# The gate matmul of both layers as seven quadrant products, with the partial sums left in PSUM, and a shorter lead in the second mixer's output projection

## The chip, the cores and the metric

One Trainium2 chip, one of its cores. The metric is the device time of one execution in microseconds (us). A core has TensorE (PE in the profile; PEld is its weight load), VectorE (DVE), ScalarE (ACT), GpSimd (POOL) and SyncE (SP, which here only issues DMAs). All of them run their own queue in order and wait on semaphores for each other. SBUF is the on-chip working memory, PSUM the eight banks into which TensorE writes.

## The reference

Two layers over 1024 tokens of width 1024. The part of the reference that the change touches, cut down:

```python
def short_conv_mixer(x, w_in, conv_w, w_out):          # layer 1 only
    gate_b, gate_c, h = jnp.split(jnp.einsum('bsd,de->bse', x, w_in), 3, axis=-1)
    z = gate_c * h
    conv = sum(conv_w[k] * zp[:, k:k + s] for k in range(CONV_WIDTH))   # zp: z padded
    return jnp.einsum('bse,ed->bsd', gate_b * conv, w_out)

for i in range(DEPTH):
    mix = ...                                           # layer 0: pooling + gMLP, layer 1: short_conv_mixer
    x = layer_norm(DEEPNORM_ALPHA * x + mix, ln1_g[i], ln1_b[i])
    hid = jnp.square(jax.nn.relu(jnp.einsum('bsd,df->bsf', x, ffn_w1[i])))
    x = layer_norm(DEEPNORM_ALPHA * x + jnp.einsum('bsf,fd->bsd', hid, ffn_w2[i]), ln2_g[i], ln2_b[i])
    gate = jax.nn.sigmoid(jnp.einsum('bsd,de->bse', x, ple_gate_w[i]))
    x = x + gate * jnp.einsum('bsk,kd->bsd', p[i], ple_w[i])
```

The last two lines are the gate stage, run once per layer: a 1024x1024 by 1024x1024 product under a sigmoid, times a product of p (1024x256) with ple_w (256x1024).

## The kernel before

Every float32 matmul is made of three: each operand is split into a high part (fp32r) and the low rest, and `product` issues high by high, low by high and high by low into one PSUM bank. ACT makes a high part (a cast), DVE or POOL makes the low part (raw minus high, a `TENSOR_TENSOR`). Eight PSUM banks form two rings of four, `bank_a` and `bank_b`.

The whole program is a list of stages made by `make_plan`; each engine walks the same list and does its own share of each stage. The order of the work on an engine is thus the order of the plan. The large products (both FFN matmuls, most of the short convolution's input projection and its output projection) are already done as seven products of quadrants where a plain scheme has eight: `m1`, `m2`, `m7`, `m6`, `m5`, `m3`, `m4`. In the output projections `m6`, `m5` and `m3` are added in PSUM on top of `m1`, and `m4` on top of `m7`. A product of these is cut into items (`prod`); DVE and ACT make an item's operands ahead in `prep` (tiles `hop_hi`, `hop_lo`, `wop_hi`, `wop_lo`), up to five items ahead, and DVE drains the banks into `resid` when a product is done (L2153, L2156).

The gate stage before (`gates`) is plain: for each of the two column halves and each of the eight token tiles, PE makes eight `product`s of the gate (24 matmuls of 128x512) into one bank of ring B and two of p (6 matmuls) into the next. ACT takes the sigmoid (`sig`), DVE scales and shifts `resid` by the layer norm's rows `gb_rows` (L2339, L2340), multiplies sigmoid and p's product (L2344) and adds them to `resid` (L2347). The weights come by DMA into `raw`, ACT makes `w_hi` or `g_hi`, POOL `w_lo` or `g_lo` (L1326). TensorE transposes (L2404) make the x operands `xt_hi`, `xt_lo` of the second token half within this stage, and those of the next stage at its end.

Of the kernel before, what the change touches and what calls it, by code (L numbers as in the profile page):

```python
# [65 lines left out]
OD_DIRECT = {2: "g11", 3: "g21"}  # L66
PLE = 256
# [20 lines left out]
class Stage:  # L88
# [30 lines left out]
    def n(self, name, k=0):  # L119
# [20 lines left out]
    "alpha": {}, "affine": {},  # L140
    "vln": {}, "stats": {}, "norm": {}, "split": {}, "square": {}, "second": {}, "wsum": {}, "slab": {}, "more": {}, "gload": {}, "gsplit": {}, "p": {}, "psum_in": {}, "psum": {}, "psum_out": {}, "lasthid": {}, "tsum": {}, "thi": {}, "t4": {}, "step": {},
# [3 lines left out]
                h="conv", ffn="aval", out="bread", wide="bread", v="bread", gate="bread", prod="flu")  # L145

# [232 lines left out]
def make_plan():  # L379
# [9 lines left out]

    def add(kind, slab=None, last=False, **args):  # L390

        if slab is not None:
            slabs.append((slab, at["piece"]))
            at["slab"] += 1
            at["piece"] += 5 if slab[0] == "gate" else 4
# [22 lines left out]
        for ring, name in (("A", "ga"), ("B", "gb")):  # L418
            for k in range(adds.get(name, 0)):
                bank = (at[name] + k) % RING  # L420
                st.bank_before[ring].append(held[ring][bank])
                held[ring][bank] = (by, at[by] + k + 1)
# [10 lines left out]
        return st  # L433

# [59 lines left out]
    def ffn(layer):  # L494
# [35 lines left out]
        for i, (form, j) in enumerate(ITEMS):  # L530
# [26 lines left out]
            if i == LAST_FORM + 4:  # L557
                add("turn_p", half=0, layer=layer)
            if i == LAST_FORM + 5:
# [19 lines left out]
    def gates(layer):  # L579
        add("more", slab=("gate", layer, 0), split_next=False, load_next=False)  # L580
        add("gate", slab=("gate", layer, 1), tiles=[0, 1], layer=layer, split_next=False, load_next=False)
        add("gload", layer=layer)
        inner = [turns("ln", 1, list(range(KT)), ln=2 * layer + 1, nested=True)]
        inner.append(add("turn_p", half=1, layer=layer, nested=True))
        add("gate", tiles=[2, 3], inner=inner, layer=layer)
        add("gsplit", item=0, layer=layer)
        add("gate", tiles=hi[:-1], layer=layer)
        add("gsplit", item=1, layer=layer)
        add("gate", tiles=hi[-1:], layer=layer)
        for _ in range(3):  # L590
            slab_end.append(("gb", at["gb"]))
        for c in (2, 3):
            add("more", slab=("gate", layer, c), split_next=False, load_next=False)
        st = add("gate", tiles=lo, col=1, layer=layer, split_next=True, load_next=True)
        if layer == 0:
            last_half("gate", "gate", layer=layer, col=1)
        else:
            add("gate", tiles=hi, col=1, layer=layer, last=True)


    def short_conv():
# [28 lines left out]
        for i, (form, j) in enumerate(OD_ITEMS):  # L630
            while nxt < len(OD_ITEMS) and (a.user_before(nxt) is None or a.user_before(nxt) < i):
# [58 lines left out]
def trunk(nc, x, p, ev_w_in, ev_pool_w, ev_pool_scale, ev_sgu_ln_g, ev_sgu_ln_b, ev_sgu_w, ev_sgu_b, ev_w_out,  # L690
# [10 lines left out]
    with ExitStack() as ctx:  # L701
# [9 lines left out]
        def at(name, shape, offset, dt=F32):  # L711
# [4 lines left out]
            if offset + size > ARENA:  # L716
# [16 lines left out]
        sig = at("sig", [P, 2, HALF], 200 * K1)  # L733
        g_hi = [at(f"g_hi{k}", [P, PIECE], a * K1, F32R) for k, a in enumerate((152, 156, 160, 164, 168, 172))]
        g_lo = [at(f"g_lo{k}", [P, PIECE], a * K1, F32R) for k, a in enumerate((154, 158, 162, 166, 170, 174))]
# [18 lines left out]
                  for k, where in enumerate((104, 114, 124, 134, 200, 202, 204))]  # L754
# [79 lines left out]
        sig_ready = sem("sig_ready")  # L834
# [33 lines left out]
        gate_step = sem("gate_step")  # L868
# [8 lines left out]
                      odstep=od_step, odcopy=od_copied)  # L877
# [1753 lines left out]
```

## Time and profile before

| | us |
|---|---|
| median of 3 runs | 2071.99 (2071.43 to 2072.64) |
| the profiled execution, its own time | 2070.66 |
| its span, first to last instruction | 2068.9 |
| PE busy | 2052.1, 99% of the span, 9437 matmuls |
| DVE busy | 1325.2, 64% |
| ACT busy | 853.9, 41% |
| POOL busy | 790.2, 38% |
| granted TensorE clock, mean | 0.999 of full speed |

Busy time counts an instruction from its start to its modelled end, so that neighbouring matmuls overlap. The profiled execution's time lies 1.76 us over its span, and 1.33 us under the median.

### The profile page before, as it was taken

What the parts mean: (1) busy time and instruction counts of PE and PEld (TensorE: products, weight loads), DVE (VectorE), ACT (ScalarE), POOL (GpSimd) and SP (SyncE); (2) the same over time, 40 slices, a digit from 0 to 9 for tenths busy, and PEclk for the clock granted to TensorE, in tenths of its full rate; (3) what the DMA queues carried; (4) which work ended last, traced back from release to release, by engine and by line L of the source; (5) the groups of instructions that cost most, each with busy time, mean ns of one, the idle gap of its engine ahead of it and who ended that gap; (6) DMA issues with size and microseconds to landing.
All of it is one profiled execution on the core that took longest, in us unless ns stands there. A gap on an engine that the chain in (4) does not pass through costs nothing. (4 is left out here: it accounts for less than half of the span.)

```text
span 2068.9 us, 25147 instructions
## 1 busy us (share of the span) xinstructions
PE 2052.1 (99%) x9437; PEld 1702.7 (82%) x9437; DVE 1325.2 (64%) x1677; ACT 853.9 (41%) x1241; POOL 790.2 (38%) x523
## 2 busy tenths in 40 slices
PE   9999999999999999999999999999999999999999
PEld 9888788888888888888878887888888888888887
DVE  4744775655666757564687769775655666666563
ACT  3112465454544334431433334655445543334430
POOL 5212157787702000212266751167877412000220
PEclk9999999999999999999999999999999999999999
DMA  5111123444589655411022238034444599554221
GB/s 189 42 62 45 38 82 137 144 161 156 197 309 390 218 201 182 141 34 41 21 88 86 87 133 299 1 122 145 150 158 142 205 382 362 185 202 153 97 87 41
DMA packets 190708, 306.05 MB, mean 148 GB/s; under 512 B 13472, under 2 KB 71932, under 8 KB 190588
## 3 DMA queue, kind: packets, MB, share of 16 engines
q1 hardware_dynamic: 189888, 304.14, 42.1%
q8 instruction: 75, 1.23, 0.2%
q14 instruction: 45, 0.37, 0.1%
q10 hardware_dynamic: 700, 0.31, 0.1%
HBM read 233.62 MB, written 70.78 MB: 147 GB/s over the span
## 5 line engine op out<-in xcount | busy, mean ns | idle before, releaser
L1326 POOL TENSOR_TENSOR w_lo<-raw,w_hi 128x512 fp32r<-128x512 f32 x92 | 131.0, 1455 | 744.0 <-ACT w_hi L1441 744.0
L1339 POOL TENSOR_TENSOR op_lo<-op_sum,op_hi 128x512 fp32r<-128x512 f32 x151 | 225.1, 1506 | 34.4 <-ACT op_hi L1643 28.5
L1608 ACT CAST hop_hi<-h_raw 128x1024 fp32r<-128x1024 f32 x124 | 130.4, 1051 | 257.0 <-PE bank_a L2367 155.4
L1643 ACT CAST op_hi<-op_sum 128x512 fp32r<-128x512 f32 x151 | 93.9, 622 | 329.5 <-POOL op_sum L1420 87.9
L2365 PE MATMUL bank_a<-wop_hi,hop_hi 128*128 128x512 f32 x576 | 224.2, 389 | 4.7 <-DVE resid L2153 4.7
L2131 DVE TENSOR_TENSOR hop_lo<-h_raw,hop_hi 128x1024 fp32r<-128x1024 f32 x124 | 152.0, 1226 | 117.5 <-ACT hop_hi L1608 117.3
L2367 PE MATMUL bank_a<-wop_hi,hop_lo 128*128 128x512 f32 x576 | 224.1, 389 | 0.0
L2366 PE MATMUL bank_a<-wop_lo,hop_hi 128*128 128x512 f32 x576 | 224.1, 389 | 0.0
L1339 POOL TENSOR_TENSOR op_lo<-w_raw,op_hi 128x512 fp32r<-128x512 f32 x115 | 164.2, 1428 | 116.4 <-ACT op_hi L1643 115.3
L2367 PE MATMUL bank_a<-xt_hi,op_lo 128*128 128x512 f32 x456 | 177.4, 389 | 0.0
L2365 PE MATMUL bank_a<-xt_hi,op_hi 128*128 128x512 f32 x456 | 177.4, 389 | 0.0
L2366 PE MATMUL bank_a<-xt_lo,op_hi 128*128 128x512 f32 x456 | 177.4, 389 | 0.0
L2365 PE MATMUL bank_b<-wop_hi,hop_hi 128*128 128x512 f32 x432 | 168.8, 391 | 0.3 <-DVE resid L2156 0.3
L2367 PE MATMUL bank_b<-wop_hi,hop_lo 128*128 128x512 f32 x432 | 168.2, 389 | 0.0
L2366 PE MATMUL bank_b<-wop_lo,hop_hi 128*128 128x512 f32 x432 | 168.1, 389 | 0.0
L2134 DVE TENSOR_TENSOR wop_lo<-w_raw,wop_hi 128x1024 fp32r<-128x1024 f32 x108 | 131.6, 1218 | 0.5
L2365 PEld LDWEIGHTS bank_a<-wop_hi,hop_hi 128*128 128x128 f32 x576 | 108.1, 188 | 28.0 <-DVE wop_lo L2134 5.5
L2365 PE MATMUL bank_a<-xt_hi,w_hi 128*128 128x512 f32 x320 | 126.8, 396 | 0.0
L2367 PEld LDWEIGHTS bank_a<-wop_hi,hop_lo 128*128 128x128 f32 x576 | 108.1, 188 | 22.4
L2366 PEld LDWEIGHTS bank_a<-wop_lo,hop_hi 128*128 128x128 f32 x576 | 108.2, 188 | 22.3
L2367 PE MATMUL bank_a<-xt_hi,w_lo 128*128 128x512 f32 x320 | 124.7, 390 | 0.0
L2366 PE MATMUL bank_a<-xt_lo,w_hi 128*128 128x512 f32 x320 | 124.6, 389 | 0.0
(243 smaller groups left out, 4879.4 us busy)
## 6 DMA issues: line engine op xcount, KB each, us to landing
w_raw<-in_ffn_w_dram SPq DMA_DIRECT2D x144, 512.0 KB, 6.8
h_raw<-h_spill SPq DMA_DIRECT2D x112, 512.0 KB, 5.2
h_spill<-h_tile SPq DMA_DIRECT2D x170, 256.0 KB, 2.1
w_raw<-in_ffn_w_dram SPq DMA_DIRECT2D x112, 256.0 KB, 3.3
w_raw<-in_od_w_in_dram SPq DMA_DIRECT2D x40, 256.0 KB, 3.3
w_raw<-in_od_w_out_dram SPq DMA_DIRECT2D x18, 512.0 KB, 7.6
raw<-in_ple_gate_w_dram SPq DMA_DIRECT2D x32, 256.0 KB, 3.5
h_spill<-h_tile2t SPq DMA_DIRECT2D x28, 256.0 KB, 2.0
```

What stands on the lines that cost most here:

```text
L1326: pool.tensor_tensor(lo, raw[:, n % NRAW, :], hi.bitcast(F32), ALU.subtract).then_inc(lo_split, 1)
L1339: pool.tensor_tensor(by_four(op_lo[s]), operand_raw(tr, b, op), by_four(op_hi[s]).bitcast(F32), ALU.subtract).then_inc(op_low, 1)
L1608: act.copy(hop_hi[k][:, :, :], h_raw[a.hop_chunk(i)][:, :, :]).then_inc(ahead_hi, 1)
L1643: act.copy(by_four(op_hi[s]), operand_raw(tr, b, op)).then_inc(op_high, 1)
L2131: dve.tensor_tensor(hop_lo[k][:, :, :], h_raw[a.hop_chunk(i)][:, :, :], hop_hi[k][:, :, :].bitcast(F32), ALU.subtract).then_inc(ahead_dve, 1)
L2134: dve.tensor_tensor(wop_lo[k][:, :, :], w2_source(a, i), wop_hi[k][:, :, :].bitcast(F32), ALU.subtract).then_inc(ahead_dve, 1)
L2365: pe.matmul(dst, s_hi, m_hi, start=first, stop=False, skip_group_check=on_top)
L2366: pe.matmul(dst, s_hi, m_lo, start=False, stop=False, skip_group_check=on_top)
L2367: return pe.matmul(dst, s_lo, m_hi, start=False, stop=last, skip_group_check=on_top)
```

## The change

It has four parts.

1. **Gate product by quadrants, in both layers.** X is cut into token halves and input halves (X11, X12 the first tokens, X21, X22 the last), the gate's weight W into B11, B12, B21, B22. Seven products of 4 tiles x 4 `product`s: m1 = X11 B11, m2 = X12 B21, m7 = S3 T3, m6 = S2 T2, m5 = S1 T1, m3 = S4 B22, m4 = X22 T4, with S3 = X11 - X21, S2 = X22 - S3, S4 = X12 - S2, S1 = X21 + X22 and T3 = B22 - B12, T1 = B12 - B11, T2 = T3 + B11, T4 = B21 - T2. DVE makes the S sums and all low parts of them (`x_step`, `x_low`), POOL the T sums and their low parts (`sums`, `lows`), ACT the high parts. Each is done in two instructions of 128x1024.
2. **Partial sums in PSUM.** m1's four banks of ring A stay and take m6, m5 and m3 on top; m4 goes on top of m7 in ring B. ACT copies the banks out after m1, m6 and m5; DVE adds ring B's banks to the copies.
3. **p's product by quadrants**: p11 between the tiles of m2, then p12, p22, p21 after m4. Both halves of p are now transposed late in the FFN. The affine work on `resid` is done for whole rows of 128x1024, four tiles early in the stage and four after S1's low part.
4. **The second mixer's output projection** prepares an item at most two ahead of the product for its first six items, where before it went as far as the operand slots allowed.

The plan and TensorE's part of the diff:

```diff
     def gates(layer):
         add("more", slab=("gate", layer, 0), split_next=False, load_next=False)
-        add("gate", slab=("gate", layer, 1), tiles=[0, 1], layer=layer, split_next=False, load_next=False)
-        add("gload", layer=layer)
...
+        first = add("gm", item=0, layer=layer)
+        gx = add("gx", source="ln", half=1, js=list(range(KT)), layer=layer, ln=2 * layer + 1, ring="B")
...
-            while nxt < len(OD_ITEMS) and (a.user_before(nxt) is None or a.user_before(nxt) < i):
+            while nxt < len(OD_ITEMS) and (i >= 6 or nxt <= i + 2) \
+                    and (a.user_before(nxt) is None or a.user_before(nxt) < i):
                 prepare(OD, nxt)
...
+GATE_ITEMS = ("m1", "m2", "m7", "m6", "m5", "m3", "m4", "p12", "p22", "p21")
...
+                def gate_tile(k, dst):
+                    h, c = places[name]
+                    w = gate_weights(layer, 1 if name in ("m2", "m6", "m3") else 0)
+                    t = slice(k * P, (k + 1) * P)
+                    for q in range(4):
+                        ins = product(dst[:, :], (xt_hi[h][:, c + q, t], xt_lo[h][:, c + q, t]),
+                                      (w[0][:, q, :], w[1][:, q, :]), q == 0 and not on_top, q == 3, on_top)
+                    return ins
...
+                if name == "m2":
+                    pe.wait_ge(unit_lo, st.need_h[0])
+                    order = (("m", 0), ("m", 1), ("m", 2), ("p", 0), ("m", 3), ("p", 1), ("p", 2), ("p", 3))
...
+                if name[0] == "m":
+                    x_part, w_part = {"m7": ("S3l1", "T3l1"), "m6": ("S2l1", "T2l1"), "m5": ("S1l1", "T1l1"),
+                                      "m3": ("S4l1", "B22l1"), "m4": ("Xl1", "T4l1")}[name]
+                    gate_x_done(pe, layer, x_part)
+                    gate_w_done(pe, layer, w_part)
```

POOL's and DVE's part (each call is two instructions of 128x1024; `add_bank`, `add11` read a bank, `gated` and `gate11` multiply by a bank and add to `resid`), and ACT's order in m6:

```diff
+                if name == "m1":
+                    sums("T3", second, second, first, ALU.subtract)
+                if name == "m2":
+                    lows("T3", 0, second)
+                    sums("T1", first, first, third, ALU.subtract)
+                    sums("T2", third, second, third, ALU.add)
+                if name == "m7":
+                    lows("T2", 1, third)
+                    gate_load_landed(pool, layer, 3)
+                    sums("T4", second, second, third, ALU.subtract)
+                if name == "m6":
+                    lows("T1", 0, first)
...
+                if name == "m1":
+                    affine(range(0, HT))
+                if name == "m2":
...
+                    x_step(g_sum[80], xt11[0].bitcast(F32), g_sum[168], ALU.subtract)
+                    x_step(g_sum[80], g_sum[80], xt11[1].bitcast(F32), ALU.add, "S3a")
+                    add11(0, 0)
...
+                    x_step(g_sum[48], g_sum[176], g_sum[80], ALU.subtract, "S3b")
+                    add11(1, 1)
+                    gate_x_done(dve, layer, "S2r1")
+                    x_low(s3[1], g_sum[80], s3[0], "S3")
+                    add11(2, 2)
+                    gate11(0, 3)
+                    add11(3, 4)
+                    for k in (1, 2, 3):
+                        gate11(k, 4 + k)
+                if name == "m7":
+                    gate_product_done(dve, st, "m2")
+                    x_step(g_part, xt12[0].bitcast(F32), g_sum[48], ALU.subtract, "S2r")
...
+                    x_low(xt11[1], g_sum[48], xt11[0], "S2")
+                    x_step(g_sum[168], g_sum[168], g_sum[176], ALU.add)
...
+                if name == "m6":
+                    gate_product_done(act, st, "m7")
+                    x_high("S1", xt_hi[1][:, 0:4, :], g_sum[168], "S1r")
+                    w_high("T1", 0, gw_raw[152])
```

**POOL in a layer's gate stage.** Before, the gate stage has POOL make the low parts of six gate pieces and of one slab, each 128x512:

```order
L1326 TENSOR_TENSOR g_lo_72<-raw,g_hi_66 128x512
L1326 TENSOR_TENSOR g_lo_73<-raw,g_hi_67 128x512
L1326 TENSOR_TENSOR g_lo_74<-raw,g_hi_68 128x512
L1326 TENSOR_TENSOR g_lo_75<-raw,g_hi_69 128x512
L1326 TENSOR_TENSOR w_lo_57<-raw,w_hi_55 128x512 x4
```

Now the same place holds 19 instructions of 128x1024 (`gw_raw_65`, `_66`, `_67` hold the T sums, in the order T3, T3 low, T1, T2, T2 low, T4, T1 low, B22 low, T4 low, and p's):

```order
L1442 TENSOR_TENSOR gw_raw_66<-gw_raw_66,gw_raw_65 128x1024 x2
L1449 TENSOR_TENSOR w_lo_56<-gw_raw_66,w_hi_54 128x1024 x2
L1442 TENSOR_TENSOR gw_raw_65<-gw_raw_65,gw_raw_67 128x1024 x2
L1442 TENSOR_TENSOR gw_raw_67<-gw_raw_66,gw_raw_67 128x1024 x2
L1449 TENSOR_TENSOR w_lo_57<-gw_raw_67,w_hi_55 128x1024 x2
L1442 TENSOR_TENSOR gw_raw_66<-gw_raw_66,gw_raw_67 128x1024 x2
L1449 TENSOR_TENSOR w_lo_56<-gw_raw_65,w_hi_54 128x1024 x2
L1449 TENSOR_TENSOR w_lo_57<-gw_raw_67,w_hi_55 128x1024 x2
L1449 TENSOR_TENSOR w_lo_56<-gw_raw_66,w_hi_54 128x1024 x2
L1476 TENSOR_TENSOR w_lo_57<-gp_raw,w_hi_55 128x1024
```

Work of 128x512 has become work of 128x1024, and six pieces plus part of a slab have become 19 instructions.

**DVE from the end of m2 to m5's operands.** Before, DVE had in this stage four instructions per tile and column half, two for the affine, the product with a bank and the addition:

```order
L2339 TENSOR_TENSOR resid<-resid,gb_rows 128x512
L2340 TENSOR_TENSOR resid<-resid,gb_rows 128x512
L2344 TENSOR_TENSOR sig<-sig,bank_b 128x512
L2347 TENSOR_TENSOR resid<-resid,sig 128x512
```

Now, after the last of p11, there stand (S4's first half in `g_part`, S2 low, S1, X22 high, X22 low, S4, S4 low, S1 low):

```order
L2172 TENSOR_TENSOR sig_76<-sig_76,bank_b 128x512
L2176 TENSOR_TENSOR resid<-resid,sig_76 128x512
L2147 TENSOR_TENSOR g_part<-xt_hi_50,g_sum_69 128x1024 x2
L2152 TENSOR_TENSOR xt_lo_52<-g_sum_69,xt_hi_50 128x1024 x2
L2147 TENSOR_TENSOR g_sum_72<-g_sum_72,g_sum_73 128x1024 x2
L2217 CAST xt_hi_51<-g_sum_73 128x1024 x2
L2220 TENSOR_TENSOR xt_lo_53<-g_sum_73,xt_hi_51 128x1024 x2
L2147 TENSOR_TENSOR g_sum_70<-g_part,xt_lo_52 128x1024 x2
L2152 TENSOR_TENSOR xt_lo_52<-g_sum_70,xt_hi_50 128x1024 x2
L2152 TENSOR_TENSOR xt_lo_53<-g_sum_72,xt_hi_51 128x1024 x2
```

m6 waits for the second of these pairs of 128x1024, m5 for the last.

**DVE in the second mixer's output projection.** Before, three items' operands (from the line with `t_od_178`) stand ahead of the drain of m1's banks:

```order
L2115 TENSOR_TENSOR t_od_178<-w_raw_163,w_raw_161 128x1024
L2131 TENSOR_TENSOR hop_lo_138<-h_raw_153,hop_hi_133 128x1024
L2134 TENSOR_TENSOR wop_lo_148<-t_od_178,wop_hi_143 128x1024
L2093 TENSOR_TENSOR w_raw_164<-w_raw_164,w_raw_157 128x1024
L2115 TENSOR_TENSOR t_od_179<-w_raw_158,w_raw_164 128x1024
L2131 TENSOR_TENSOR hop_lo_134<-h_raw_154,hop_hi_129 128x1024
L2134 TENSOR_TENSOR wop_lo_144<-t_od_179,wop_hi_139 128x1024
L2117 TENSOR_TENSOR w_raw_159<-w_raw_159,t_od_178 128x1024
L2131 TENSOR_TENSOR hop_lo_135<-h_raw_155,hop_hi_130 128x1024
L2134 TENSOR_TENSOR wop_lo_145<-w_raw_159,wop_hi_140 128x1024
L2153 TENSOR_TENSOR resid<-resid,bank_a 128x512 x4
```

Now one of them does:

```order
L2426 TENSOR_TENSOR t_od_177<-w_raw_162,w_raw_160 128x1024
L2442 TENSOR_TENSOR hop_lo_137<-h_raw_152,hop_hi_132 128x1024
L2445 TENSOR_TENSOR wop_lo_147<-t_od_177,wop_hi_142 128x1024
L2464 TENSOR_TENSOR resid<-resid,bank_a 128x512 x4
L2404 TENSOR_TENSOR w_raw_163<-w_raw_163,w_raw_156 128x1024
L2426 TENSOR_TENSOR t_od_178<-w_raw_157,w_raw_163 128x1024
L2442 TENSOR_TENSOR hop_lo_133<-h_raw_153,hop_hi_128 128x1024
L2445 TENSOR_TENSOR wop_lo_143<-t_od_178,wop_hi_138 128x1024
L2467 SCALAR_TENSOR_TENSOR resid,row_sum<-resid,bank_b 128x512 x4
```

The drain of m1's banks moved ahead of the operands of two items.

## Rows read from the trace of the kernel before

**Rows 1.** The page: busy time and instructions of each engine.

```profile
PE 2052.1 (99%) x9437; PEld 1702.7 (82%) x9437; DVE 1325.2 (64%) x1677; ACT 853.9 (41%) x1241; POOL 790.2 (38%) x523
```

**Rows 2.** Busy time by stretch; stretches: gate stage 0, next stage, output projection, gate stage 1.

```profile
core 0: us, PE busy (x) PEld busy (x) DVE busy (x) ACT busy (x) POOL busy (x), PEclk, DMA share, GB/s
880.80:998.30 117.50, 117.28 (x555) 97.68 (x553) 67.86 (x104) 32.72 (x54) 21.20 (x14) 1.00 0.11 32
998.30:1023.40 25.10, 25.10 (x130) 21.18 (x128) 21.69 (x31) 8.39 (x17) 6.56 (x4) 1.00 0.14 42
1950.80:2068.90 118.10, 113.85 (x522) 94.22 (x520) 62.11 (x95) 27.02 (x43) 15.28 (x10) 0.99 0.16 58
```

**Rows 3.** Timeline of PE: one tile of gate stage 0, transposes at its end.

```profile
start us, us, engine line op out<-in xcount [idle before <-releaser]
974.22 0.39 PE L2365 MATMUL bank_b<-g_hi,xt_hi 128*128 128x512 f32 x1
...
981.02 0.39 PE L2365 MATMUL bank_b<-g_hi,xt_hi 128*128 128x512 f32 x1
...
987.83 1.91 PE L2404 MATMUL bank_a<-ident,resid 128*128 128x128 f32 x16
```

**Rows 4.** Waits of PE in the whole program.

```profile
PE bank_a L2365 <- DVE resid L2153: 4.7, 2, 3.0
PE bank_b L2365 <- DVE sig L2344: 0.4, 2, 0.2
```

**Rows 5.** Instructions of a line: DVE and POOL, 128x1024, the other engine quiet.

```profile
L2117 DVE TENSOR_TENSOR w_raw<-w_raw,t x32: 1212/1218/1226, 676.8 to 1924.6; 128x1024 f32<-128x1024 f32 x32
L1366 POOL TENSOR_TENSOR w_raw<-w_raw,w_raw x16: 2389/2400/2918, 610.7 to 1740.7; 128x1024 f32<-128x1024 f32 x16
```

**Rows 6.** Timelines of DVE and POOL, both at 128x1024 at once.

```profile
292.11 5.49 DVE L2000 TENSOR_TENSOR t_raw<-xt_hi,t_raw 128x1024 f32<-128x1024 f32 x2 [8.56 <-PE bank_a L2367]
297.63 3.31 DVE L2009 TENSOR_TENSOR t_lo<-t_raw,t_hi 128x1024 fp32r<-128x1024 f32 x1
...
293.12 6.73 POOL L1393 TENSOR_TENSOR t_lo<-t_raw,t_hi 128x1024 fp32r<-128x1024 f32 x2
```

**Rows 7.** Timeline of DVE, gate stage 0, start of it and beside POOL's 912.58 to 922.37.

```profile
884.70 1.53 DVE L1946 TENSOR_SCALAR resid<-resid,neg_mean,rstd 128x1024 f32<-128x1024 f32 x2
...
914.34 1.77 DVE L2339 TENSOR_TENSOR resid<-resid,gb_rows 128x512 f32<-128x512 f32 x1
...
917.74 0.67 DVE L2344 TENSOR_TENSOR sig<-sig,bank_b 128x512 f32<-128x512 f32 x1
```

**Rows 8.** Timeline of DVE in the output projection: operands, then the drain.

```profile
1258.78 1.22 DVE L2117 TENSOR_TENSOR w_raw<-w_raw,t_od 128x1024 f32<-128x1024 f32 x1
...
1261.10 1.23 DVE L2134 TENSOR_TENSOR wop_lo<-w_raw,wop_hi 128x1024 fp32r<-128x1024 f32 x1
1262.24 2.47 DVE L2153 TENSOR_TENSOR resid<-resid,bank_a 128x512 f32<-128x512 f32 x4
```

**Rows 9.** Timeline of ACT: a cast of 128x1024.

```profile
1229.15 1.05 ACT L1608 CAST hop_hi<-h_raw 128x1024 fp32r<-128x1024 f32 x1
```

**Rows 10.** Timeline: PE's first transposes of `ident`, the same sixteen later.

```profile
1.58 3.67 PE L2372 MATMUL bank_b<-ident 128*128 128x128 f32 x16 [1.58 <-POOL ident L1318]
...
7.29 1.91 PE L2372 MATMUL bank_b<-ident 128*128 128x128 f32 x16
```

**Rows 11.** The end: last matmul, and stretches by granted clock.

```profile
2064.48 0.39 PE L2367 MATMUL bank_b<-w_hi,hid_lo 128*128 128x512 f32 x1
...
2066.00:2067.00 1.00, 0.00 (x0) 0.00 (x0) 0.48 (x1) 0.00 (x0) 0.00 (x0) 0.92 0.00 0
2067.00:2068.90 1.90, 0.00 (x0) 0.00 (x0) 0.00 (x0) 0.00 (x0) 0.00 (x0) 0.50 0.37 138
```

**Rows 12.** Timeline of DVE: x operands at the start of the next stage.

```profile
998.76 0.69 DVE L1789 TENSOR_TENSOR xt_lo<-tmp,xt_hi 128x512 fp32r<-128x512 f32 x1
...
1001.75 3.47 DVE L1789 TENSOR_TENSOR xt_lo<-tmp,xt_hi 128x512 fp32r<-128x512 f32 x2
```

More of the change, by code:

```diff
@@ L558, in ffn @@
                 add("turn_p", half=0, layer=layer)
+                add("turn_p", half=1, layer=layer)
             if i == LAST_FORM + 5:
@@ L580, in gates @@
         add("more", slab=("gate", layer, 0), split_next=False, load_next=False)
-        add("gate", slab=("gate", layer, 1), tiles=[0, 1], layer=layer, split_next=False, load_next=False)
-        add("gload", layer=layer)
[L583 to L594, printed above, removed]
-        if layer == 0:
-            last_half("gate", "gate", layer=layer, col=1)
-        else:
-            add("gate", tiles=hi, col=1, layer=layer, last=True)
+        first = add("gm", item=0, layer=layer)
+        gx = add("gx", source="ln", half=1, js=list(range(KT)), layer=layer, ln=2 * layer + 1, ring="B")
+        first.inner = [gx]
+        turned[1] = "gb", at["gb"]
+        items = [first]
+        for i in range(1, len(GATE_ITEMS)):
+            if GATE_ITEMS[i] == "p21" and layer == 0:
+                nested = turns("gate", 0, [0, 1, 2, 3], nested=True)
+            args = dict(slab=("gate", layer, 1)) if i == 1 else {}
+            items.append(add("gm", item=i, layer=layer, load_next=GATE_ITEMS[i] == "m4",
+                             split_next=GATE_ITEMS[i] == "p22", **args))
+            if GATE_ITEMS[i] in ("m4", "p22"):
+                slab_end.append(("gb", at["gb"]) if GATE_ITEMS[i] == "m4" else ("ga", at["ga"]))
+        if layer == 0:
+            items[-1].inner = [nested]
+            turns("gate", 0, [4, 5, 6, 7])
+        for st in items:
+            st.heads = {GATE_ITEMS[s.item]: s for s in items}
+            st.gx = gx
+        gx.heads = items[0].heads
     def short_conv():
@@ L944, in staged @@
         def staged(st, k):
-            early = st.source == "ln" and st.ln % 2 == 0 or st.source == "gate" and st.half == 1
+            early = st.source == "ln" and st.ln % 2 == 0 or st.source == "gate"
+            if st.kind == "turn" and st.source == "gate" and st.half == 0 and st.js[k] >= 4:
+                return g_turn[:, st.js[k] - 4, :]
             if st.kind == "turn" and early and st.js[k] < 4:
@@ L1301, in stage @@
                     load_gb(ln1_g[0], ln1_b[0], D)
-                if st.kind == "gate" and st.layer == 1:
-                    c = slice(st.col * HALF, (st.col + 1) * HALF)
-                    for k, t in enumerate(st.tiles):
-                        sp.wait_ge(x_new, st.xnew + k + 1)
-                        sp.dma_start(out_v[:, t, c], resid[:, t, c]).then_inc(out_done, 16)
             for st in plan:
@@ L1555, in stage @@
                     split_high(st.cur + 1, st.piece, 4, end)
-                fifth = st.split_next and st.cur + 1 < n_slabs and slabs[st.cur + 1][0][0] == "gate"
                 if st.kind == "split":
@@ L2408, in stage @@
             def stage(st):
-                if st.first and st.cur > 0 and not (st.kind == "more" and slabs[st.cur][0][2] >= 2):
+                if st.first and st.cur > 0:
                     pe.wait_ge(lo_split, st.n("piece"))
```

442 lines of the change are left out of this document (336 added, 106 removed).

## The prediction

> **What bounds the kernel now.** I read the page first: PE is busy 2052.1 us of a span of 2068.9, DVE 64%, ACT 41%, POOL 38% [rows 1]. Then the stretches: in gate stage 0 PE is busy 117.28 of 117.50 us, in gate stage 1 113.85 of 118.10 with the end of the program inside, and POOL has only 21.2 and 15.3 us of work there [rows 2]. PE's timeline gives the price of its work: from 974.22 to 981.02 it issues 30 matmuls, 6.80 / 30 = 0.2267 us each; a `product` is three of them, 0.68, a gate tile of four products 2.72, a p tile of two 1.36 [rows 3]. Last the waits: inside the gate stage PE waits 0.4 us on DVE in all, and in front of the second mixer's on-top products twice for the drain of `bank_a` (L2153), 4.7 us together, the longer 3.0 [rows 4]. So a matmul less is 0.2267 us less, as long as the others keep up. Whether they do is the whole question, for the change moves work to DVE and POOL.
>
> **Matmuls removed.** A layer's gate has 2 x 8 tiles x 24 = 384 matmuls before and 7 x 4 x 12 = 336 after; p keeps 96. Two layers: 96 x 0.2267 = **-21.8 us**.
>
> **What the new operands cost alone.** DVE needs 1.22 us for 128x1024, POOL 2.40 [rows 5]. In a layer POOL gets 19 such, DVE 22 (and two casts) for the S sums, 16 for the affine work, and the additions to `resid`. Added up engine by engine, DVE has some 94 us of work and POOL 45 in a stage of 106.5 us (117.5 less 10.9): either would fit.
>
> **What they cost together.** The trace holds one place where both engines work on 128x1024 in SBUF at the same time [rows 6]: two of POOL's take 6.73 us instead of 4.80, and DVE's third takes 3.31 instead of 1.22. 6.73 / 2 = 3.36 is one instruction of each in turn, of which DVE's is 1.15 (its spacing alone, three from 1258.78 to 1262.24 [rows 8]) and POOL's the other 2.2. They don't overlap at all. At half the size it is the same: affine instructions of 128x512 take 1.77 beside POOL, while the one that reads a bank stays at 0.67 [rows 7]; two `xt_lo` take 3.47 where one alone is 0.69 [rows 12]. So I walk the stage with one rule from these rows: DVE's instructions with two SBUF inputs and all of POOL's take turns, one by one; those that read a bank run beside POOL. On one shared lane the stage then has, per layer, 19 x 2.25 + 38 x 1.15 and some 16 x 0.7 of additions, 98 us of 106. That is too full for a chain in which PE needs certain operands early. The Trainium skill ("SBUF — State Buffer", section "SBUF: two separate sides") says as much: DVE with two SBUF inputs and GpSimd share a port pair as an exclusive lock held for the whole instruction. The trace agrees (6.73 us for two); a kernel planned by the sum of each engine alone would be told by it that it is planned wrongly.
>
> **The walk of one layer**, in us from PE's first gate matmul. DVE is free at 5.4 (880.8 to 886.2, the end of the norm [rows 7]). Without waits PE would come to m2 at 14.3 (four tiles 10.9, transposes 3.4), to m7 at 30.6, to m6 at 41.5.
> - m2 and p11: banks of ring B come free by ACT's copies of the transposes and by DVE's `add11`, which stand in DVE's order between S sums and the low part of S3. The first tile waits 1.0; the one that needs the bank of the third waits 5.3, because that `add11` stands behind S3's second low part, ready at 33.5 when the lane has also carried T3's two low parts. m7 waits 0.9. m6 is thus wanted at 41.5 + 7.2 = 48.7.
> - m6 needs S2's low part. Ahead of its end DVE has 8 affine and 12 S instructions on the lane and 4 additions, and POOL has T3, T3 low, T1, T2, T2 low and T4, 12 in all: 5.4 + 20 x 1.15 + 4 x 0.7 + 12 x 2.25 = 58.2, and about 1.2 in which neither could hold it: 59.4. **Wait 10.8.**
> - m5 is wanted at 59.5 + 10.9 = 70.4 and needs T1's low part from POOL. It follows on S2: DVE's S1, X22 high and low and S4 (7.8), then ACT in its order S4, S1 (two), T1, spaced by about one [rows 9], 4.9 more, then POOL's two T1 instructions with an affine instruction of DVE between them, 5.4 with the start: 77.6. **Wait 7.2.**
> - m3, m4 and p's products find their operands: B22's low part ends at 84.5 for 88.4, T4's at 95.1 for 99.3. In p's products DVE needs 1.41 per tile (a bank read and an addition) against PE's 1.36, which banks in hand absorb.
> Together 1.0 + 5.3 + 0.9 + 10.8 + 7.2 = 25.2 per layer, **+50.4**. The same walk without taking turns has 1.7 per layer. With the two durations 2 to 4% lower or higher it gives 23.3 to 27.4. Where the cover is: before, it was the smallness of POOL's work here (21 us), and it is gone.
>
> **Behind layer 0.** The next stage's x operands 4 to 7 now come after p21's additions, and its weights' low parts by POOL fall on them: DVE is 21.69 of 25.10 us busy there already [rows 2], and `xt_lo` shows 1.7 each under POOL [rows 12]. The walk has PE wait 4.4 for the fifth. **+4.4**; bounds 0 (they are ready) and 7 (all four pairs at 1.7).
>
> **p's second half** is turned in the FFN's end: four DVE instructions of 128x512, 2.4 to 3.8 us, ahead of the last item's operands, which have slack of items ahead. I take 0.3 per layer, **+0.6**; bounds 0 and 1.9 each. The casts and copies that ACT gets are costed at nothing: they lie under the idle 59% of ACT [rows 1], and those on the path are counted above.
>
> **The output projection.** DVE ran operands of three items ahead of the drain of m1: three instructions of 1.15 each and then 2.47 of drain [rows 8], and PE waited 3.0 for it, and 1.7 at the other such place. Now one item stands ahead; the drain comes two items, 2 x 3.46 = 6.9, earlier, more than either wait. About 0.5 of the later one may stay, as the items held back then come later: 4.7 - 0.5 = **-4.2**; bounds 0 (an item's operands become late instead) and -4.7.
>
> **The clock.** PE ran at full clock throughout. After its last matmul (2064.48) the granted clock is 0.92 from 2066 to 2067 and 0.50 from there [rows 11], so a wait of 10.8 or 7.2 reaches the level of 1.2 GHz. The first sixteen transposes, after idleness, take 3.67 against 1.91 later [rows 10]: 1.8 per restart. After m6's wait it is hidden, since m5 waits for POOL, not for PE. After m5's it counts: 2 x 1.8 = **+3.6**; bounds 0 and 7 (both restarts of both layers).
>
> **The sum**, against the profiled execution's 2070.66 (span 2068.9 and 1.8 around it; it is 1.3 below the median): 2070.7 - 21.8 + 50.4 + 4.4 + 0.6 - 4.2 + 3.6 = 2103.7. The median of the new kernel may lie at it or 1 above. I say **2103**. The likeliest case's own range is 2088 to 2113: waits of 20 to 27 per layer, and the other terms' bounds in part.
>
> **Rivals.**
> 1. Less bunching, about 2092. POOL's T4 needs a third load that starts when T2 is done (45.0); I had it landed by 52.6. Comes it later, T4's two instructions fall behind S2's low part, which is then 4.5 earlier, and m5 with it. 2103 - 2 x 4.5 = 2094, 2090 if the order helps at S3 too. For it: DMA share here is 0.11, so it should be early [rows 2], which speaks against. Chance 0.15.
> 2. The other side: the lane does not decide, 2049. If DVE got several turns for POOL's one, or the turns were only taken where inputs collide, the walk has 1.7 of waits per layer and no restart: 2070.7 - 21.8 + 3.4 + 0.6 - 4.2 = 2048.7. Against it are all three places of [rows 6], [rows 7] and [rows 12], which show one by one; for it, that POOL's instructions wait for ACT's casts and so may be spread better than I have them. It decides from where waits and restarts of both layers, with what follows them, fall under 26 us in total, half of my sum. Chance 0.10, and 0.03 for about 2072, no change.
> 3. Worse, 2115 and up: the lane also holds the x operands of the short convolution, or PE stays at half clock through more of m6 and m5, or semaphores between DVE's linked instructions add 0.1 to each. 60 instructions x 0.1 x 2 = 12. Chance 0.10.
> The forecast itself keeps 0.62. Against 2071.99, +-0.2% (4 us) is about what a measurement of this kernel can tell from no change: faster 0.10, same 0.03, slower 0.87. The range to hold 8 in 10 leaves out the other side's 0.13 and part of the worse end: 2080 to 2114.
>
> **What would show it.** PE has 9437 - 96 = 9341 matmuls. In its waits there are, per layer, about 11 us on DVE's `xt_lo` ahead of m6, about 7 on POOL's `w_lo` ahead of m5, about 5 on `sig` or a bank in p11. DVE's S instructions beside POOL show 3.3 us and POOL's 3.4, not 1.22 and 2.40; PE's granted clock falls in both gate stages. The drain's 4.7 us falls under 1. Wrong I would be if POOL's instructions stood at 2.4 beside DVE's at 1.2, or if S2's low part ended before PE had done m7.

## The result, and the profile after

The changed kernel takes 2106.81 us (median of 4 runs, 2104.98 to 2108.48) against 2072.07 before (2071.43 to 2072.64): a ratio of 1.0169, 95% interval 1.0156 to 1.0182. It is 35 us slower, against 31 forecast, inside the range.

The page of the changed kernel: its span, busy time with instructions, and the granted clock in 40 slices.

```profile
span 2104.0 us, 25031 instructions
...
PE 2048.2 (97%) x9341; PEld 1694.8 (81%) x9341; DVE 1419.2 (67%) x1685; ACT 891.5 (42%) x1283; POOL 876.2 (42%) x541
...
PEclk9999999999999999999999999999999999999989
```

TensorE has 96 matmuls less and is busy 3.9 us less than in [rows 1], for a span 35.1 us longer. The clock, 0.999 of full speed in the mean before and 0.989 now, shows as 8 tenths in slice 39, in gate stage 1; in gate stage 0 it stays at 9 tenths or more in each slice (52.6 us long), at a mean of 0.93 in the stretch below.

Waits of PE in the changed kernel: engine, tile and line, what it waited for, us in total, times, the longest.

```profile
PE bank_a L2654 <- DVE xt_lo L2152: 15.9, 2, 8.4
PE bank_b L2654 <- DVE sig L2168: 10.3, 4, 5.0
PE bank_a L2654 <- POOL w_lo L1449: 10.1, 2, 5.5
PE bank_b L2654 <- DVE resid L2467: 4.3, 1, 4.3
PE bank_a L2654 <- DVE xt_lo L1986: 2.8, 1, 2.8
...
PE bank_a L2654 <- DVE resid L2464: 0.4, 1, 0.4
```

The 4.7 us in front of the projection's products [rows 4] have shrunk to 0.4 (L2464), but 4.3 stand at a later drain (L2467). New are three kinds of wait in each gate stage: on S2's low part ahead of m6 (`xt_lo` L2152, 8.4 in the longer case), on the reader of a bank in p11 (`sig`, 5.0) and on T1's low part ahead of m5 (`w_lo`, 5.5). Together 36.3 us. The 2.8 is the fifth x operand of the stage behind gate stage 0.

Busy time by stretch: gate stage 0, the next stage, gate stage 1 with the end.

```profile
core 0: us, PE busy (x) PEld busy (x) DVE busy (x) ACT busy (x) POOL busy (x), PEclk, DMA share, GB/s
882.60:1011.60 129.00, 109.94 (x480) 89.71 (x479) 104.67 (x94) 49.16 (x70) 63.12 (x23) 0.93 0.18 62
1011.60:1035.00 23.40, 20.59 (x108) 17.02 (x107) 19.04 (x32) 8.33 (x16) 6.22 (x4) 0.93 0.14 46
1975.00:2104.00 129.00, 107.30 (x456) 86.88 (x454) 104.72 (x92) 44.14 (x62) 56.74 (x19) 0.92 0.22 77
```

Beside [rows 2], PE is now busy for 110 of 129 us in gate stage 0, not 117 of 117.5; POOL has gone from 21 to 63 us and DVE from 68 to 105. Part of what looks busy is an instruction that waits for its turn, as the timelines show.

DVE in gate stage 0: S3's low part, the reader of p11's bank, S4's first half, S2's low part, and S1.

```profile
909.68 6.11 DVE L2152 TENSOR_TENSOR xt_lo<-g_sum,xt_hi 128x1024 fp32r<-128x1024 f32 x2
915.72 0.67 DVE L2168 TENSOR_TENSOR sig<-sig,bank_b 128x512 f32<-128x512 f32 x1
...
926.91 6.73 DVE L2147 TENSOR_TENSOR g_part<-xt_hi,g_sum 128x1024 f32<-128x1024 f32 x2
933.68 6.52 DVE L2152 TENSOR_TENSOR xt_lo<-g_sum,xt_hi 128x1024 fp32r<-128x1024 f32 x2
940.12 2.35 DVE L2147 TENSOR_TENSOR g_sum<-g_sum,g_sum 128x1024 f32<-128x1024 f32 x2
```

POOL in the same stage: T3's low part, T1 and T2, T2's low part, T4, and then T1's and B22's low parts.

```profile
908.41 6.30 POOL L1449 TENSOR_TENSOR w_lo<-gw_raw,w_hi 128x1024 fp32r<-128x1024 f32 x2 [11.39 <-ACT w_hi L1717]
914.68 11.77 POOL L1442 TENSOR_TENSOR gw_raw<-gw_raw,gw_raw 128x1024 f32<-128x1024 f32 x4
926.40 6.16 POOL L1449 TENSOR_TENSOR w_lo<-gw_raw,w_hi 128x1024 fp32r<-128x1024 f32 x2
932.52 6.60 POOL L1442 TENSOR_TENSOR gw_raw<-gw_raw,gw_raw 128x1024 f32<-128x1024 f32 x2
952.23 12.73 POOL L1449 TENSOR_TENSOR w_lo<-gw_raw,w_hi 128x1024 fp32r<-128x1024 f32 x4 [13.11 <-ACT w_hi L1717]
```

S4 and S2's low part, four instructions of DVE, take 13.2 us (926.91 to 940.12) while POOL's four, from 926.40 to 939.1, take 12.7: 3.3 for one of each, as in [rows 6]. As soon as POOL has stopped, S1's two instructions take 2.35 together. From 939.1 to 952.23 POOL is idle, until ACT has made T1's high part, and DVE's additions and low parts take 1.2 each. So the wait ahead of m5 comes mostly from the order of the work; of what stands between S2's low part and m5, only POOL's last two instructions, 6.1 for 4.8 alone, share the lane with DVE. The four of T1's and B22's low parts beside affine work take 3.18 each. The reader of a bank at 915.72 takes 0.67 with POOL at work.

PE ahead of p11's third tile, m6 and m5.

```profile
916.45 0.80 PE L2654 MATMUL bank_b<-w_hi,hid_hi 128*128 128x512 f32 x1 [4.96 <-DVE sig L2168]
...
940.26 0.79 PE L2654 MATMUL bank_a<-w_hi,xt_hi 128*128 128x512 f32 x1 [8.44 <-DVE xt_lo L2152]
...
958.42 0.77 PE L2654 MATMUL bank_a<-w_hi,xt_hi 128*128 128x512 f32 x1 [5.46 <-POOL w_lo L1449]
958.99 0.63 PE L2655 MATMUL bank_a<-w_lo,xt_hi 128*128 128x512 f32 x1
959.41 0.63 PE L2656 MATMUL bank_a<-w_hi,xt_lo 128*128 128x512 f32 x1
```

The wait for S2's low part ends at 940.26, that is 57.6 after the first gate matmul (882.62; the walk had 59.5), the wait for T1's low part at 958.42, which is 18.2 later (the walk: 18.1). After it PE's matmuls are 0.43 us apart, where 0.227 is the spacing at full clock: that is the level of 1.2 GHz.

DVE in the second mixer's projection: the first operand work behind m1, then four instructions of the last operands and the start of the last drain.

```profile
1269.13 1.22 DVE L2404 TENSOR_TENSOR w_raw<-w_raw,w_raw 128x1024 f32<-128x1024 f32 x1
...
1304.54 2.32 DVE L2442 TENSOR_TENSOR hop_lo<-h_raw,hop_hi 128x1024 fp32r<-128x1024 f32 x1
1306.79 2.30 DVE L2445 TENSOR_TENSOR wop_lo<-w_raw,wop_hi 128x1024 fp32r<-128x1024 f32 x1
1309.01 2.92 DVE L2428 TENSOR_TENSOR w_raw<-w_raw,t_od 128x1024 f32<-128x1024 f32 x1
1311.86 1.21 DVE L2442 TENSOR_TENSOR hop_lo<-h_raw,hop_hi 128x1024 fp32r<-128x1024 f32 x1
...
1327.79 0.68 DVE L2467 SCALAR_TENSOR_TENSOR resid<-resid,bank_b 128x512 f32<-128x512 f32 x1
```

POOL at that time.

```profile
1300.78 7.23 POOL L1420 TENSOR_TENSOR w_lo<-raw,w_hi 128x512 fp32r<-128x512 f32 x4 [51.75 <-ACT w_hi L1574]
1308.09 2.78 POOL L1511 TENSOR_SCALAR gb_rows<-gb_rows 128x2048 f32<-128x2048 f32 x1
```

Three of DVE's operand instructions take 2.3, 2.3 and 2.9 us where the next one shows 1.21: POOL makes the low parts of the next weights and scales `gb_rows` just then. In the kernel before, POOL did this from 1280.38 to 1287.96 on its own clock, when DVE stood idle for PE.

### The profile page after: what moved, and what is told of

Read it like the earlier page. It is cut to its first block, busy times and chain, and to the rows that moved or that the text cites. A ratio compares the mean times of both kernels' runs of the same rounds, so it can differ in the third digit from the quotient of the medians.

```text
span 2104.0 us, 25031 instructions
## 1 busy us (share of the span) xinstructions
PE 2048.2 (97%) x9341; PEld 1694.8 (81%) x9341; DVE 1419.2 (67%) x1685; ACT 891.5 (42%) x1283; POOL 876.2 (42%) x541
## 3 DMA queue, kind: packets, MB, share of 16 engines
q8 instruction: 74, 1.21, 0.2%
## 4 chain that ended last, share of the span: by engine, by line
PE 82%; DVE 10%; issue 3%; POOL 3%; ACT 1%; DMA 0%; SPq 0%; DVEq 0%; ACTq 0%; POOLq 0%
PE bank_a L2654 16%; PE bank_a L2656 15%; PE bank_a L2655 15%; PE bank_b L2654 11%; PE bank_b L2656 11%; PE bank_b L2655 11%; POOL op_lo L1433 2%; DVE xt_lo L2152 1%; PE bank_b L2693 1%; DVE hop_lo L2442 1%; POOL op_sum L1553 1%; DVE wop_lo L2445 1%; PE bank_a L2693 1%; DVE g_part L2147 1%; POOL w_lo L1449 1%
## 5 line engine op out<-in xcount | busy, mean ns | idle before, releaser
L1420 POOL TENSOR_TENSOR w_lo<-raw,w_hi 128x512 fp32r<-128x512 f32 x84 | 121.5, 1477 | 688.2 <-ACT w_hi L1574 688.1
```

Source lines behind the costliest of these rows:

```text
L1420: pool.tensor_tensor(lo, raw[:, n % NRAW, :], hi.bitcast(F32), ALU.subtract).then_inc(lo_split, 1)
```

## The experiments

All times are medians; "before" was timed on the same chip each time and stayed at 2071.7 to 2071.9. The changed kernel has its one median, 2106.81, so a difference from it also carries its own spread of 2105.0 to 2108.5. In the lines of the profile an experiment's source lines lie a few off those of the changed kernel.

### The two parts apart

**e1_gate_only**: the changed kernel, with the projection's lead as it was.

```diff
-            while nxt < len(OD_ITEMS) and (i >= 6 or nxt <= i + 2) \
-                    and (a.user_before(nxt) is None or a.user_before(nxt) < i):
+            while nxt < len(OD_ITEMS) and (a.user_before(nxt) is None or a.user_before(nxt) < i):
```

> The change with the output projection's lead as it was before (items prepared as far as slots allow), the rest changed. Theory A (DVE bounds this projection, so the edit only moves PE's waits to a later drain): the projection costs PE the 5.5 us of waits that it cost before in place of the 5.0 us plus 1.5 us of matmuls at the lower clock of the changed kernel, so 2105.3 us, 2104 to 2107. Theory B (the step of the prediction: the edit takes 4.2 us away): 2111 us.

2104.48 us (ratio 1.0159, 1.0145 to 1.0173). Its wait at the drain of m1's banks:

```profile
PE bank_a L2653 <- DVE resid L2463: 3.0, 1, 3.0
```

**e2_od_only**: the kernel before with the same lines the other way round.

> The kernel before with the shorter lead of the first six items alone. Theory A (only moved, with the low parts of the next weights by POOL falling on DVE's late operands): PE's waits of 3.0 and 1.7 us at the drain of m1's banks go, one of about 4.3 us at the last drain comes, 2073.6 us, 2072 to 2075. Theory B: 2067.9 us and no wait over 1 us there.

2073.03 us (ratio 1.0006, 0.9997 to 1.0014). Its wait at the last drain of the projection; the one at m1's banks is 0.5 now:

```profile
PE bank_b L2366 <- DVE resid L2157: 4.7, 1, 4.7
```

Both come out as theory A says. The shorter lead removes nothing by itself: alone it gives +1.4 us, which can't be told from none, and without it the changed kernel is 2.3 us shorter, with intervals that overlap; the 4.2 us of the prediction are excluded by both. The loss is that of the gate stages, with the stage behind the first.

### Is it the lane that DVE and POOL share?

**e3_pool_narrow**: POOL's T sums and low parts in the gate stages done for 16 of each 512 columns. The rest of these weights is left out; all instructions and waits stay.

```diff
-                        pool.tensor_tensor(pair_of(dst, m), pair_of(left, m), pair_of(right, m), op)\
+                        pool.tensor_tensor(pair_of(dst, m)[:, :, 0:16], pair_of(left, m)[:, :, 0:16],
+                                           pair_of(right, m)[:, :, 0:16], op)\
... the low parts in the same way
```

> The changed kernel with POOL's T sums and low parts in the gate stages done for 16 of each 512 columns only; the rest of these weights is left out, each instruction and each wait stays. Theory A (the lane that DVE and POOL share makes the waits): with POOL's part of it gone DVE's S instructions take 1.2 us, the waits ahead of m6 and m5 go, 1 to 2 us per layer are left, 2062 us, 2058 to 2067. Theory B (DVE's chain of S instructions with its semaphores is too long by itself): the wait ahead of m6 stays at 6 us or more, and the time is 2090 us or above. Theory C (POOL's own chain of 2.4 us each is what is late, not the sharing): the waits on POOL ahead of m5 go, those on DVE stay, 2095 us.

2055.71 us (ratio 0.9921, 0.9908 to 0.9935), 51 less than the changed kernel. PE has no wait over 0.4 us left in either gate stage. DVE's S2 low part in this run, then POOL's T1 and T2:

```profile
917.98 2.42 DVE L2154 TENSOR_TENSOR xt_lo<-g_sum,xt_hi 128x1024 fp32r<-128x1024 f32 x2
```

```profile
905.51 2.85 POOL L1442 TENSOR_TENSOR gw_raw<-gw_raw,gw_raw 128x32 f32<-128x32 f32 x4
```

S2's low part takes 2.42 where it took 6.52, the same instructions with the same semaphores. Theories B and C fall: with POOL's share gone DVE's waits go too. It came out 6 us under the expected 2062; I had left 1 to 2 us per layer of waits, which weren't there, and had not counted that all matmuls at the lower clock in the gate stages (10.6 us, of the 13.8 in the table below) go with the waits. The run takes POOL's own duration away along with its turns, so by itself it does not weigh the two; the next run does, for the wait ahead of m6.

**e9_t4_narrow**: only T4's two sums narrowed; that sum is left out but for 16 columns.

```diff
+                        n = slice(0, 16 if form == "T4" else HALF)
-                        pool.tensor_tensor(pair_of(dst, m), pair_of(left, m), pair_of(right, m), op)\
+                        pool.tensor_tensor(pair_of(dst, m)[:, :, n], pair_of(left, m)[:, :, n],
+                                           pair_of(right, m)[:, :, n], op)\
```

> The changed kernel with T4's two sums alone done for 16 of each 512 columns; the rest of that sum is left out. Theory A (every instruction of POOL ahead of S2's low part on the lane costs PE 2.2 us): the wait ahead of m6 falls from 8.4 and 7.5 by 4.4 in each layer, nothing else changes, 2098 us, 2096 to 2100. Theory B (only the sum of what overlaps at the very end counts, DVE is then late by its own instructions): it falls by 2.2 or less, 2102 us or more.

2096.29 us (ratio 1.0120).

```profile
PE bank_b L2656 <- DVE sig L2170: 10.4, 4, 5.0
PE bank_a L2656 <- POOL w_lo L1451: 9.9, 2, 5.4
PE bank_a L2656 <- DVE xt_lo L2154: 7.7, 2, 4.0
```

T4 isn't used before m4, and PE waits for none of it ahead of m6. Yet without its work the wait ahead of m6 falls from 15.9 to 7.7 in both layers together, 4.1 each, 2.05 for each instruction of POOL. The other two kinds of wait stay. That is the lane itself, theory A. For the wait ahead of m6, what counts is what POOL puts ahead of S2's low part on it, whether PE needs it then or not.

### Order on the lane

**e4_late_affine**: of the first four tiles' affine work only the half row that p11 needs stands early.

```diff
                 if name == "m1":
-                    affine(range(0, HT))
+                    affine(range(0, HT), 0)
...
+                if name == "m3":
+                    affine(range(0, HT), 1)
+                    affine(range(HT, TT))
```

> The changed kernel with the affine work put later: of the first four tiles only the half row that p11 needs stands early (8 instructions of 128x512 for 8 of 128x1024), the rest stands after m7's banks are added. Theory A: 4.8 us of DVE's work and its turns leave the shared lane ahead of S2, so m6 starts 4.6 us sooner and the waits in p11 and ahead of m6 fall by as much together, the wait ahead of m5 by about 1; near m4 one of 1 to 2 us comes back. 8 us less in all, 2099 us, 2096 to 2102. Theory B (the early affine is covered by PE's m1 and the chain starts with the third load of weights or with the turned x): m6 starts as before, 2107 us.

2101.16 us (ratio 1.0135, 1.0120 to 1.0151), 5.7 less where 8 were expected.

```profile
PE bank_a L2659 <- DVE xt_lo L2152: 18.1, 2, 9.1
PE bank_a L2659 <- POOL w_lo L1449: 8.3, 2, 4.7
...
PE bank_b L2659 <- DVE sig L2172: 4.1, 4, 1.4
PE bank_b L2659 <- DVE g_sum L2172: 3.4, 2, 1.7
```

The wait in p11 fell from 10.3 to 4.1 in all, the one ahead of m6 rose from 15.9 to 18.1, since PE comes to it earlier, and the one ahead of m5 fell by 1.8; 3.4 came back where DVE reads m7's banks late (`g_sum`). The direction of theory A holds. In the traces m6 starts 4.2 sooner after the stage's first matmul (4.6 were expected) and m5 5.1, and 1.7 per layer come back at that bank, for which I had allowed 1 to 2. Layer 0 thus gains 4.1, as expected. Layer 1 gains 2.0, and 1.1 of what it lacks is the clock: thirteen slow matmuls follow m5's wait there, where the changed kernel had eight.

**e5_order**: e4, and m5's operands first on ACT and DVE.

```diff
... ACT's part
                 if name == "m6":
                     gate_product_done(act, st, "m7")
-                    x_high("S1", xt_hi[1][:, 0:4, :], g_sum[168], "S1r")
                     w_high("T1", 0, gw_raw[152])
+                    x_high("S1", xt_hi[1][:, 0:4, :], g_sum[168], "S1r")
+                    x_high("S4", xt_hi[0][:, 4:8, :], g_sum[56], "S4b")
... DVE's: S4 and S1's low part ahead of X22's high and low parts
```

> The kernel with the late affine work (e4), and besides the operands of m5 made first: ACT casts T1, S1, S4 in place of S4, S1, T1, and DVE makes S1's low part ahead of X22's and S4's. Theory A (the wait ahead of m5 is the length of the order DVE, ACT, POOL after S2, on the shared lane): T1's low part no longer waits for five casts and S4; the wait of 3.8 to 4.9 ahead of m5 falls by about 2 per layer, some of it coming back ahead of m3; 2098 us, 2094 to 2100. Theory B (POOL is held by its own work until then, so ACT's order is covered): the time of e4, 2101 us.

2092.62 us (ratio 1.0100, 1.0086 to 1.0113), 8.5 less than e4 where 3 were expected.

```profile
PE bank_a L2658 <- DVE xt_lo L2152: 18.1, 2, 9.0
...
PE bank_a L2658 <- ACT g_sum L1701: 2.8, 2, 1.5
```

The wait on `w_lo` ahead of m5 is gone; what is left there is 1.3 and 1.5 on ACT's copy of m6's first bank. So this wait was mostly one of order, and m5 starts 1.9 sooner. I had not counted the clock: with a wait of 1.3 and 1.5 in place of 3.6 and 4.7, m5 starts at full clock, which is 1.5 and 2.6 more.

### The clock

**e7_fill**: filler matmuls in PE's waits, into banks that are free. They add products that don't belong there, so the output is not the reference's.

```diff
+                        if position == 6:
+                            fill(free_bank("A", st.heads["m6"], 0), 18)
...
+                    if name in ("m6", "m5"):
+                        fill(free_bank("A", st, 0), 30 if name == "m6" else 18)
                     gate_x_done(pe, layer, x_part)
...
+            def fill(dst, count):
+                for _ in range(count):
+                    pe.matmul(dst[:, :], hid_hi[:, 0, 0:P], hid_hi[:, 0, 0:HALF], start=False, stop=False,
+                              skip_group_check=True)
```

> The changed kernel with TensorE given filler matmuls of 128x512 in its three waits of each gate stage: 18 ahead of p11's third tile, 30 ahead of m6, 18 ahead of m5, each into a bank that is free; they add products that don't belong to the result, so the output is not the reference's. They are fewer than the waits hold. Theory A (of the matmuls at the lower clock only those after m5 count, since what PE loses before is taken from the next wait): m5's first eight to twelve matmuls run at 0.227 us, 3.8 us less in both layers together, 2103 us, while the idle time of PE plus the fillers ahead of m6 and m5 is about 1 to 2 us longer than before. Theory B (all matmuls at the lower clock count): 9.5 us less, 2097 us. Theory C (the clock falls all the same): 2107 us.

2103.14 us (ratio 1.0145), 3.7 less. Stretch 905 to 970 (p11 to m5) in this run, then in the changed kernel, with the columns of the stretches above:

```profile
905.00:970.00 65.00, 58.25 (x250) 46.05 (x250) 63.79 (x41) 22.49 (x28) 43.66 (x14) 1.00 0.17 55
```

```profile
905.00:970.00 65.00, 45.94 (x174) 36.01 (x173) 63.76 (x42) 22.40 (x28) 43.35 (x14) 0.87 0.17 57
```

And PE in the run with fillers, at the start of m6 and of m5.

```profile
940.95 0.50 PE L2654 MATMUL bank_a<-w_hi,xt_hi 128*128 128x512 f32 x1 [2.35 <-DVE xt_lo L2152]
...
959.21 0.47 PE L2654 MATMUL bank_a<-w_hi,xt_hi 128*128 128x512 f32 x1 [0.51 <-issue]
959.52 0.39 PE L2655 MATMUL bank_a<-w_lo,xt_hi 128*128 128x512 f32 x1
```

The clock stays at 1.00 instead of 0.87, and m5's matmuls are 0.23 apart from the second on. Yet m6 starts at 940.95 and m5 at 959.21, no sooner than at 940.26 and 958.42. The fillers do not hold m5 up: T1's low part ends at 959.11 here. Matmuls at half clock ahead of the next wait cost nothing, for m6 and m5 wait for DVE and POOL; only those behind m5 are gained, 2.3 in layer 0 and 1.4 in layer 1 by the traces. Theory A.

### The projection

**e6_od_slab_later**: the kernel before with the shorter lead, and the next slab's weights split two items later.

```diff
-            if i == 7:
+            if i == 9:
                 add("slab", layer=OD, load_next=True, split_next=True)
```

> The kernel before with the shorter lead, and ACT's casts of the next slab of weights (w_hi) put behind the casts of the last two items, so that POOL's low parts of it start later. Theory A (the 4.7 us that PE waits for the last drain are POOL's turns among DVE's operands): these operands take 1.2 us again, the drain is done 4 us sooner, PE waits under 1 us and keeps its clock: 2067 us, 2065 to 2069. Theory B (DVE is late by its own work): the wait stays at 4 us or more, 2073 us.

2067.18 us (ratio 0.9976, 0.9966 to 0.9985): 4.7 us faster than before. DVE's operand instructions, then POOL's low parts, then PE's two waits in the projection:

```profile
1285.06 1.22 DVE L2132 TENSOR_TENSOR hop_lo<-h_raw,hop_hi 128x1024 fp32r<-128x1024 f32 x1
1286.26 1.23 DVE L2135 TENSOR_TENSOR wop_lo<-w_raw,wop_hi 128x1024 fp32r<-128x1024 f32 x1
```

```profile
1293.79 5.58 POOL L1327 TENSOR_TENSOR w_lo<-raw,w_hi 128x512 fp32r<-128x512 f32 x4 [64.27 <-ACT w_hi L1442]
```

```profile
PE bank_a L2366 <- DVE resid L2154: 0.5, 1, 0.5
PE bank_b L2366 <- DVE resid L2157: 0.5, 1, 0.5
```

POOL's work now begins at 1293.79, as DVE ends its operands and goes to drains, which read banks. The instructions are back at 1.22 and the wait of 4.7 at 0.5, and the time is 5.9 under e2's. The later slab without the shorter lead was not run.

**e8_combined**: e5 and e6's line on the changed kernel.

> The changed kernel with late affine work and m5's operands first (e5), and the next slab's casts later (e6). If the two gains are apart, as the shared lane says: e5's 2092.6 us less the 5.5 us of wait and 1.8 us of lower clock in the projection, plus 0.6 that e6 has left there, 2086 us, 2084 to 2088. If POOL's later low parts hold up something behind the projection in this kernel, 2088 or more.

2087.19 us (ratio 1.0074, 1.0057 to 1.0091). The two gains add up, within 1.2 us of the 2086 expected. It is 20 us better than the change as made, and still 15 slower than before. The fastest of all that ran in full is e6: the old gate stage with the shorter lead and the later slab.

## Why the prediction came out as it did

The sum against the two traces, in us. Matmuls at the lower clock were found by the starts of PE's rows, 0.33 to 0.52 apart: 93 after and 20 before, 0.19 each over the full-clock spacing. The first matmul after a wait is not among them; after six of the eight long waits the next one starts 0.56 to 0.59 behind it, after two 0.31.

| term | forecast | measured |
|---|---|---|
| matmuls removed | -21.8 | -21.8 (9341 of them) |
| waits in the gate stages | +50.4 | +36.3 |
| matmuls at the lower clock | +3.6 | +13.8 |
| the first matmul after each wait, and small | 0 | +3.6 (the rest) |
| the stage behind layer 0 | +4.4 | +2.8 |
| p's second half | +0.6 | +0.4 |
| the projection's waits | -4.2 | 0.0 (4.7, then 4.3 + 0.4) |
| sum, on the span | +33.0 | +35.1 |

**Right, with its mechanism.** DVE's instructions with two SBUF inputs and POOL's take turns: e9 shows it for the wait ahead of m6; e3 fits it for the others, but takes POOL's own time away too. The places are as forecast, p11, m6 and m5, and nothing in the gate stage waits elsewhere for more than 0.4 us. p11's wait was forecast at 5.3 and is 5.0. The Trainium skill's rule of an exclusive lock for the whole instruction ("SBUF — State Buffer", section "SBUF: two separate sides") holds here nearly: POOL's instruction takes 3.1 to 3.3 beside DVE's where it takes 2.40 alone, and taking POOL's away brings DVE's 6.52 back to 2.42 for two. "They don't overlap at all" was a little too strong. One of each alone would be 1.15 and 2.38 (POOL's 4.76 for two), 3.5 together, where the pair shows 3.3, so some 0.2 us does overlap. The walk had that in its 2.25 for POOL's turn, and e9 measures 2.05.

**Mis-sized: the waits, by 14 us.** The 1.0 ahead of m2 and the 0.9 ahead of m7 weren't there (0.2 at most), and S2's low part came 1.9 earlier; PE came to it 0.5 and 1.4 later than the walk had it, with slow matmuls behind p11's wait: 8.4 and 7.5 for 10.8. For m5 the walk had the chain right (18.2 for 18.1) but let PE run m6 at full clock. With m6's first matmuls at 0.43 PE comes 1.8 and 2.7 later to the wait, which is 5.5 and 4.6 for 7.2.

**Mis-sized: the clock, by 10 us in the table, but not in the result.** I charged one restart per layer at 1.8 and argued that the others hide in the next wait. e7 shows that this is so: keeping the clock gives 3.7 back, against 3.6 forecast. In the two traces, though, the hidden ones stand as slow matmuls and as that much less wait. The two errors above are largely one thing entered twice; taken together, waits and clock were forecast at 54.0 and came to 50.1, or 53.7 with the first matmuls after a wait. That this comes so near is partly luck. From the stage's first matmul to the fifth x operand behind it the changed kernel takes 139.7 and e3, which has no waits in the stage, 113.7; from gate stage 1's first matmul to the end it is 131.1 and 106.1. The gate stages' waits and clock thus cost 51.0, not 54.0, chiefly because S2's low part came 1.9 earlier in each layer. The clock term in turn left out what happens outside the gate stages, 1.2 us behind the 2.8 and 1.5 behind the 4.3, and the two errors cancel. What the whole sum is off by, 2.1, is the projection's 4.2 less what the small terms came in under.

**Wrong: the step on the output projection.** "The drain comes two items, 2 x 3.46 = 6.9, earlier, more than either wait" is true of that drain (3.0 and 1.7 are 0.4 now). (The 6.9 was too little: by the traces the drain starts 4.8 after the first of these operands and not 13.1, for one of the two items has four instructions and not three.) What failed is the next sentence, that only about 0.5 stays. The items held back aren't fewer. DVE takes 61.2 us from the first of these operands to the end of the last drain (1269.13 to 1330.3), busy without a gap to 1321, and took 61.8 before (1249.10 to 1310.9), 4.0 of them idle at one place, waiting for the tiles of PE's m5 (1281 to 1287). DVE bounds this stretch, so PE waits for it at the first drains or at the last. That the 4.0 us of idleness, filled now, didn't turn into a gain is POOL's doing: DVE's work shifted under POOL's low parts, and 4.1 went there (2.32 + 2.30 + 2.92, less three times 1.15). I had used the lane's rule in the gate stage and not here. e6 takes that away, and the gain is there: 4.2 forecast, 4.7 measured in the time.

**The rivals.** The first (less bunching, 2092) missed: T4's load had landed and T4 ran ahead of S2's low part. e9 shows its price to be right, 4.1 per layer for 4.5. The other side needed waits and restarts under 26 us and met 50. Its 2049 is near what e3 shows with POOL's work all but gone, 2056; over it are the projection's 4.3 and the 2.8 behind layer 0 with their slow matmuls, less the 3.4 of waits that it had left in. The worse side did not come: PE stayed at the lower clock for at most 13 matmuls after any wait.

What stays open: the 2.8 us behind gate stage 0. The trace has POOL's low parts from 1015.15 to 1021.4 and DVE's two casts for this operand at 2.90 in place of 0.92, which would be the lane again, with casts. By the starts of DVE's rows these casts and the two additions ahead of them lose 2.1 and 0.6, an estimate that makes up the 2.8; no run took it apart, and e3, which left this work of POOL as it was, still has the 2.8.

## What to carry to other kernels

Before work is moved to an idle POOL, add DVE's instructions with two SBUF inputs and POOL's into one queue and walk it to the operands that TensorE needs first; 38% and 64% busy before the change were no sign of room. Work of either engine that is needed late (T4, half the affine rows, the next weights' low parts) costs its full turn if it stands ahead of what is needed early, so its place matters more than its amount. A stage's order can cost as much as its lane: m5 waited for a cast that ACT had put behind four others, and moving it took the wait on POOL away (e5). And a wait removed in front of an engine that bounds the stretch comes back at its next hand-over, unless that engine's own idle time is what gets filled.

## What the runs showed of the hardware that was not expected

- Waits of 1.3 to 1.7 us did not bring TensorE's clock down (e5, m5 and m7's bank). The wait behind gate stage 0, 2.75 us in the changed kernel and in e1, was followed by six matmuls at about 0.43 in the one and by none in the other. Before the change, a wait of 3.0 us in the projection left the matmuls at full spacing, and in e1 the same wait was followed by thirteen slow ones. So the clock's answer to a wait of about 3 us is not the same each time.
- After waits of 3.6 to 9 us 5 to 13 matmuls of 128x512 ran at 0.43 us spacing, 1.0 to 2.6 us in all, whatever the wait's length (8.4 gave 1.2, 5.0 gave 1.2 and 2.1).
- Casts of DVE with one input are held by POOL too: two of 128x512 at 2.90 us beside POOL, 0.92 without.
